# Attention and feed-forward of a one-layer decoder on one Trainium2 core: two score tiles ahead of the decode scores, decode values one tile sooner, and a wait for constants moved to the logits

## What is computed

```python
u = rmsnorm(h); proj = u @ w_in              # RWKV part and q, k, v of 8 heads x 64
q, k = rope(q), rope(k)
# prompt: causal attention, three dilated branches (128,1) (512,4) (2048,16), merged by softmax of their lse
att = merge([branch(q, k, v, window, dil) for window, dil in DILATED])
# sample group: the same branches over 2048 cached positions and the 8 new rows
h += concat(rwkv_out, rmsnorm(att)) @ w_out
h += moe(rmsnorm(h))                         # 4 groups x 8 experts, top-1 group, top-2 experts
h += sigmoid(rmsnorm(h) @ ple_gate_w) * (p @ ple_proj)
y = rmsnorm(h)
```

## Time and profile before

| | before |
|---|---|
| median of 3 runs | 1780.62 us (1776.17 to 1783.87) |
| the profiled execution, its own time | 1773.52 us |
| its span, first to last instruction | 1771.7 us |
| mean granted TensorE clock | 0.952 |
| PE busy | 1628.2 us, 92% of the span |
| DVE busy | 671.9 us, 38% |
| ACT busy | 434.1 us, 25% |
| attention block, four head pairs | about 638 to 1050 us of the span |
| feed-forward, sums to experts | from 1050 us |

### The profile page before, as it was taken

The page is one execution under the profiler, slowest core; times in us unless marked ns, Lnnn a source line. Parts: engine busy times, 40 slices in busy tenths (PEclk is TensorE's granted clock), DMA queues, the critical chain, the costliest instruction groups (busy, mean ns, idle before and its releaser), DMA issues. The chain is left out here.

```text
span 1771.7 us, 34951 instructions
## 1 busy us (share of the span) xinstructions
PE 1628.2 (92%) x15296; PEld 1143.5 (65%) x15296; DVE 671.9 (38%) x1631; ACT 434.1 (25%) x891; POOL 55.6 (3%) x57
## 2 busy tenths in 40 slices
PE   7999999989988889998989879999999999995997
PEld 4566675775675656675757654555888888883443
DVE  5365564464463213425151442234411111112564
ACT  4413214214212202304141231112111111111344
POOL 0000000000000000000000000000100000002110
PEclk9899998998997889999999989999999999997999
DMA  5000000000010043304242472004799999986321
GB/s 183 27 27 14 26 17 26 14 16 13 15 41 20 3 196 144 156 26 168 107 180 120 190 277 94 36 36 156 277 367 367 367 373 363 366 308 217 116 83 42
DMA packets 57597, 246.90 MB, mean 139 GB/s; under 512 B 7520, under 2 KB 18016, under 8 KB 47712
## 3 DMA queue, kind: packets, MB, share of 16 engines
q1 hardware_dynamic: 45632, 201.61, 30.4%
q0 software_dynamic: 7200, 26.22, 4.0%
q10 hardware_dynamic: 4608, 16.78, 2.3%
HBM read 210.70 MB, written 33.88 MB: 138 GB/s over the span
## 5 line engine op out<-in xcount | busy, mean ns | idle before, releaser
L448 PE MATMUL bank<-h,w 128*128 128x352 f32 (+1 forms) x528 | 183.2, 496 | 6.3 <-DVE xb L1007 6.3
L1760 PEld LDWEIGHTS bank<-cache,we 128*128 128x128 f32 x1536 | 175.1, 192 | 13.6 <-issue 10.5
L1760 PE MATMUL bank<-cache,we 128*128 128x128 f32 x1536 | 175.6, 275 | 2.8 <-DVE cache L2029 2.8
L2029 DVE COPY cache<-bank 128x512 f32<-128x512 f32 x64 | 41.2, 686 | 288.7 <-PE bank L1747 288.7
L448 PEld LDWEIGHTS bank<-h,w 128*128 128x128 f32 x528 | 100.7, 199 | 64.1 <-DVE xb L1007 7.6
L1251 PE MATMUL bank<-h,w 128*128 128x352 f32 (+1 forms) x384 | 120.9, 478 | 5.5 <-POOL qd L1236 5.5
L1691 PE MATMUL bank<-cache,mixed 128*128 128x512 f32 x256 | 113.0, 601 | 6.3 <-DMA mixed<-in_pad_a 6.3
L2296 PE MATMUL bank<-we,unT 128*128 128x512 f32 x256 | 113.1, 600 | 1.4 <-DVE unT L2247 1.4
L1251 PEld LDWEIGHTS bank<-h,w 128*128 128x128 f32 x384 | 74.3, 194 | 50.3 <-POOL qd L1236 6.1
L1691 PEld LDWEIGHTS bank<-cache,mixed 128*128 128x128 f32 x256 | 48.8, 193 | 65.2 <-issue 58.9
L2296 PEld LDWEIGHTS bank<-we,unT 128*128 128x128 f32 x256 | 48.7, 193 | 59.6 <-issue 57.8
(11 more groups left out here) (407 smaller groups left out, 2524.0 us busy)
## 6 DMA issues: line engine op xcount, KB each, us to landing
we<-in_weg SPq DMA_DIRECT2D x24, 1024.0 KB, 5.3
we<-in_weu SPq DMA_DIRECT2D x24, 1024.0 KB, 9.1
we<-in_wed SPq DMA_DIRECT2D x24, 1024.0 KB, 11.8
cache<-in_kcj SPq DMA_DIRECT2D x4, 5120.0 KB, 15.9
cache<-in_vcj SPq DMA_DIRECT2D x4, 5120.0 KB, 15.2
y_rows<-cache ACTq DMA_DIRECT2D x32, 512.0 KB, 8.8
cache<-in_weg SPq DMA_DIRECT2D x8, 1024.0 KB, 5.3
cache<-in_weu SPq DMA_DIRECT2D x8, 1024.0 KB, 8.5
```

Of the source, the lines that this page charges most:

```text
L448: mm = pe.matmul(out[:, 0:w], w3[:, KIND[q], kd, :], g.uT[:, kd, a:a + w], start=(kd == 0), stop=(kd == KD - 1))
L1760: mm = pe.matmul(bank[6 + e % 2][:, 128 * (2 * a + f):128 * (2 * a + f) + CAP], w[:, k, 128 * f:128 * f + 128], xT[e % 2][:, k, :], start= ...
L2029: last = dve.tensor_copy(xT[e % 2][:, 4 * c:4 * c + 4, :].rearrange("p k q -> p (k q)"), bank[4 + c][:, :])
```

## The change

In attention, PE's wait for `q_done` moves to the end of the projection, and the scores of tiles 0 and 1 are issued there, ahead of the decode scores. Since transposes write banks 0 and 1, which hold decode scores, PE waits before tile 0's transposes for a new semaphore `d_read`, which DVE raises with its second decode read. DVE softens tiles 0 and 1 ahead of the decode scores. ACT takes the exponentials of tiles 0 and 1 first and the decode exponential behind the copy of tile 0's first slot. The decode values are issued at i = 6 instead of i = 7, that is between the transposes of tile 6 and the values of tile 5. In the feed-forward, PE's wait for the constants moves from before the projection to before the first logits, at t = 2.

```diff
                 def decode_scores(j):
                     pe.wait_ge(s["qd_done"], j + 1)
-                    pe.wait_ge(s["q_done"], 2 * j + 2)
                     pe.wait_ge(s["k_in"], 16 * (j + 1))
...
                     project(j)
+                    pe.wait_ge(s["q_done"], 2 * j + 2)
+                    scores(j, 0)
+                    scores(j, 1)
                     decode_scores(j)
-                    scores(j, 0)
                     for i in range(8):
-                        if i + 1 < 8:
+                        if 1 <= i < 7:
                             scores(j, i + 1)
+                        if i == 0:
+
+                            pe.wait_ge(s["d_read"], j + 1)
                         turn(j, i)
-                        if i == 7:
+                        if i == 6:
                             decode_values(j)
                         if i:
                             values(j, i - 1)
...
-                    act.wait_ge(s["d_raised"], j + 1)
-                    act.activation(dscore[:, 0:NSEL + TS], dscore[:, 0:NSEL + TS], ACT.Exp, bias=dntop[:, 0:1], accum_out=dtotal[:, 0:1]).then_inc(s["d_exped"], 1)
-                    for i in range(8):
+
+                    def exponents(i):
                         for hh in range(2):
...
+                    exponents(0)
+                    exponents(1)
+                    for i in range(8):
+                        if i >= 2:
+                            exponents(i)
                         for hh in range(2):
                             for x in at["turn", i, hh]:
                                 if x % 2 == 0:
                                     turned_out(act, j, x)
+                        if i == 0:
+                            act.wait_ge(s["d_raised"], j + 1)
+                            act.activation(dscore[:, 0:NSEL + TS], dscore[:, 0:NSEL + TS], ACT.Exp, bias=dntop[:, 0:1], accum_out=dtotal[:, 0:1]).then_inc(s["d_exped"], 1)
...
-                        dve.tensor_tensor_reduce(out=dscore[:, a:a + w], in0=in0, in1=in1, scale=SCALE, scalar=-3e38,
-                                                 op0=ALU.add, op1=ALU.max, accum_out=dtop[:, n:n + 1])
+                        last = dve.tensor_tensor_reduce(out=dscore[:, a:a + w], in0=in0, in1=in1, scale=SCALE, scalar=-3e38,
+                                                        op0=ALU.add, op1=ALU.max, accum_out=dtop[:, n:n + 1])
+                        if n == 1:
+                            last.then_inc(s["d_read"], 1)
...
                     rotate(j)
+                    soften(j, 0)
+                    soften(j, 1)
                     decode_soften(j)
-                    soften(j, 0)
                     for i in range(8):
                         if i == 5:
                             normalise(j, 0)
                         for hh in range(2):
-                            if i + 1 < 8:
+                            if 1 <= i < 7:
                                 soften(j, i + 1, (hh,))
...
                 mm.then_inc(s["summed"], 1)
-                pe.wait_ge(s["consts"], 16 * len(LOADS))
                 for t in range(TT):
                     project(t)
                     if t >= 1:
                         turn(t - 1)
                     if t == 2:
                         pe.wait_ge(s["meaned"], 1)
+                        pe.wait_ge(s["consts"], 16 * len(LOADS))
                     if t >= 2:
                         logit(t - 2)
```

More of the change, by code:

```diff
@@ L2431 @@
                  "s_qk s_neg s_exp s_rt s_slot s_free0 s_free1 s_pv s_oev sq_done "
-                 "d_scored d_raised d_exped d_valued d_pick",
+                 "d_scored d_read d_raised d_exped d_valued d_pick",
     feed_forward="summed meaned rooted gained projected evicted added zeroed squared f_meaned f_rooted consts xnorm turned evac logits lev "
```

## The result

The changed kernel takes 1761.05 us (median of 4 runs, 1758.33 to 1767.19), the kernel before 1780.53 (4 runs). The ratio is 0.9895, 95% interval 0.9866 to 0.9924, that is 13.5 to 23.9 us less. The forecast was 1756.9 (1748 to 1767).

The account below looks back on a forecast made before the run. TensorE (PE) was busy 92% of the span, so only its idle time and clock could be won. Attention 18.2 plus constants 5.5 made 23.7 us off the median 1780.6, giving 1756.9 us, range 1748 to 1767.

Parts of the forecast that it names:

- Scores ahead: Attention pairs: prompt scores before decode scores shorten PE's gap from 3.53 to about 1.4 us; 18.2 us gained in all.
- next in line: Attention, behind the shortened gap: VectorE's decode work, copies and softening set when tile 4's scores start, at 804.3 in j=1.
- The clock: Attention gaps: PE's clock stays up around the new gap of about 1.4 us; decides 8 of the 18 us.
- Constants: Start of the feed-forward: PE's whole 6.26 us wait before the output projection goes, 5.5 us after 0.8 for clock.
- cold start: Output projection: PE starts at the low clock, costing 0 to 1.1 us more than before; 0.8 taken.
- Decode values at tile 6: Attention: decode values run ahead of tile 5's values; gain 0, bounds -0.4 and +0.4 us a pair.
- earlier wout loads: After pair j=3: the eight wout loads go out some 4 us earlier; effect 0.
- low clock that stays: Rival, attention gaps: the clock still drops in some or all pairs; gains 10 + 5.5, 1765.1 us; chance 0.17.
- gap that moves: Rival, tile 2: VectorE or ScalarE gives back 2.5 us of each pair; 1767.1 us; chance 0.08.
- wait for the V cache: Rival, decode values: they wait for V's load, slower; 1789 us if a load takes 36 us; chance 0.02.

Follow-up runs that it names:

- e6: Changed kernel with ScalarE's decode exponential behind the copies of tile 3 instead of tile 0; one run, 12.27 us from projection to tile 4's scores, unchanged.
- e7: Changed kernel with d_scored raised for each bank, so VectorE softens early banks while PE still makes later ones; median 1755.36 us, ratio 0.9883 to the kernel before.
- e4: Kernel before with three useless matmuls filling the gap ahead of tile 0's transposes in each pair; ratio 0.9955 to the kernel before.
- e5: Changed kernel with PE waiting for the whole decode softening (d_raised) instead of two reads; one run, 13.3 or 14.8 us from projection to tile 4's scores.
- e1: Kernel before with only PE's wait for the constants moved to the logits; ratio 0.994 to the kernel before.
- e3: Kernel before with only the decode values moved to tile 6; ratio 0.9995 to the kernel before.
- e9: Changed kernel with the second half of the load of x behind the wout loads instead of ahead; ratio 0.985 to the kernel before.
- e10: Changed kernel with the decode values back at tile 7; ratio 0.9863 to the kernel before.
- e8: As e7, and at tile 5 VectorE copies the transposed slot out before softening tile 6; ratio 0.9859 to the kernel before.
- e2: Changed kernel with only the new order of scores, softening and exponentials, its two other parts undone; ratio 0.9893 to the kernel before.
- e11: Kernel of e8 with the split load of x of e9; median 1752.22 us, ratio 0.9832 to the kernel before.

## Why the prediction was right, point by point

- **Scores ahead.** Forecast 5.1, 5.1, 3.9, 4.1 us; the stretches give 4.9, 4.9, 3.7, 4.0, in all 17.5 instead of 18.2. The point that it named as next in line, VectorE's chain, is the one (no idle time in it; e6 and e7). The chain came out at 12.27 us instead of 12.1; the term was over-sized by 0.7, nothing in it wrong.
- **The clock.** The forecast gave it 8 of 18 us. e4 shows 8.1 us won by the clock alone in the old order. In the new one it may be worth less: where e5's clock fell, it cost 1.5 us a pair, 6 in four. The step rested on one row, a gap of 1.46 us at full clock, and e5 shows that a gap of 2.46 would have made it a toss; that the new gap lay on the safe side was no more than likely. The rule of the Trainium skill that speaks against it (transposes don't count as busy, TensorE: Matmul & The Clock Gate, Part 4: PE-mode transpose) did not bite: the gap of 1.43 us is followed by transposes, and the clock stayed at 1.00 in every pair.
- **Constants.** Forecast 6.26 less 0.8 for the cold start, 5.5; measured 5.4 in the changed kernel, 6.5 in e1 (1.0 of it chance). Here the reason was incomplete. I took the wait for one on the constants alone; e3 shows that half of it was the wout loads ahead of them in the queue.
- **Decode values at tile 6.** This step failed. I wrote "Gain 0, bounds -0.4 and +0.4 a pair", and that PE is busy in both places. It is so in the first three pairs. In the last one PE reaches this code while the loads of V, rw and x are still draining, and halts: 1.6 us lost, outside the bounds; in its place the runs showed a fetch of instructions held up by the backlog (e9, e10). It is also where the forecast's 23.7 us and the trace's 16.1 + 5.4 = 21.5 part, with 0.7 for the reordering. The earlier wout loads, which I set at nothing, gave e3 3.4 us and the changed kernel none.
- **The rivals.** The low clock that stays and the gap that moves did not occur. Neither did a wait for the V cache.
- **The figures.** By the stretches the change gives 21.5 us, by the medians 19.5, against 23.7 forecast; the 2 us between the first two are within the scatter of the runs. Two figures of the prediction don't follow from its own terms. The lower end of the range should be 1780.6 - 24.9 - 4 = 1751.7, not 1748. And a gain of 5.1 us on pairs 102 us apart gives 96.9, not 98; measured are 97.05. The measured median lies inside either range.

## What to carry to other kernels

A short gap in front of TensorE can cost more by the clock than by its length alone (here another 1.4 to 2.6 us behind a gap of 3.5), and a filler of useless matmuls tells the two apart. Work pulled ahead should leave the smallest release condition behind (two reads instead of all, or one signal a bank). And when a stage gets shorter, ask which transfers, issued by the clock of another stage, are now still on the way.

## What was not expected of the hardware

**A backlog of loads halts TensorE without any semaphore.** With 11,648 KB of loads issued together in the last pair PE stopped at the same instruction in four kernels (the changed one, e6, e7, e8), for 1.3, 0.9, 2.8 and 3.2 us, and each time went on within 0.3 us of the landing of the last load. In each of them a fetch of instructions started 0.9 us late or more, when the bulk of the loads had passed. PE never stopped there where the loads issued ahead had landed by then (e2, e3, e5, e9, e10, e11); in e5 the longer gaps had put PE just behind the backlog.

**The same code takes up to 16 us more or less.** From the start to the first attention projection, which none of these kernels changes, the thirteen profiles took 638 to 654 us. Three of them, PE over this stretch: before, changed kernel, and e9 (columns: stretch, length, PE busy with count, granted clock, DMA share, GB/s):

```profile
0.00:638.00 638.00, 572.73 (x8528) 0.92 0.10 32
```

```profile
0.00:652.00 652.00, 580.11 (x8528) 0.91 0.09 31
```

```profile
0.00:638.00 638.00, 568.38 (x8528) 0.93 0.10 32
```

PE's busy time is 573, 580 and 568 us for the same 8528 instructions, and the mean clock goes with it (0.92, 0.91, 0.93). That is 7 of the 14 us between the first two; the other 7 are more idle time of PE, whose cause I didn't look into. The block has many short waits, and that one of them brings the clock down in some runs and not in others, as in e5, fits the figures but isn't shown for this block. The spread of 16 us is nearly as large as the reordering's 17.7 and larger than the other parts of this change. A difference of spans between two profiles says little here, and stretches with the same start say much.
